# A hybrid attention and mixture-of-experts block: the attention's order of work, its score buffers and the form of eight output products

## The reference, cut to what matters

```
h    = rmsnorm(x) @ w_in                     # split: 4 x 512 columns for the recurrence, 3 x 512 for the attention
o_a  = head_rmsnorm(hgrn2(...)) * silu(hg)   # gated linear recurrence, 4 heads of 128
o_b  = head_rmsnorm(dilated_attention(...))  # 8 heads of 64, causal, softmax over masked scores
x    = x + concat(o_a, o_b) @ w_out          # w_out: 1024 x 1024
h2   = rmsnorm(x)
x    = x + top-4-of-32 experts(h2)           # each expert: 1024 x 2048 up, clamped SwiGLU, 1024 x 1024 down
out  = rmsnorm(x)
```

## Time and profile before

| | |
|---|---|
| median of 3 runs | 1307.71 us |
| the profiled execution's own time | 1308.46 us |
| its span, first to last instruction | 1306.6 us |
| PE busy, share of the span | 96% |
| DVE, ACT, POOL busy | 41%, 18%, 10% |
| granted TensorE clock, mean | 0.988 of full |
| data read from memory | 441.46 MB |

### The profile page before, as it was taken

One profiled execution on the slowest core, in us unless ns is written; L12 is line 12 of the kernel. 1 busy time (PEld: TensorE's weight loads), 2 busy tenths in 40 slices (PEclk: granted clock), 3 DMA queues, 4 the chain that ended last, 5 costly groups with the idle time before them and its releaser, 6 DMA issues.

```text
span 1306.6 us, 33478 instructions
## 1 busy us (share of the span) xinstructions
PE 1248.9 (96%) x14751; PEld 726.3 (56%) x14752; DVE 538.1 (41%) x1045; ACT 238.5 (18%) x485; POOL 135.8 (10%) x144
## 2 busy tenths in 40 slices
PE   6999999999999999999999999999999999999994
PEld 5888876675357565555444455444445454545442
DVE  5767646566424524223242333333333333242424
ACT  6364424421011111010010100010000000010102
POOL 0000001100022221221010101001010101010002
PEclk9999999998999999999999999999999999999997
DMA  9523219027899999999999999999999999999993
GB/s 294 163 65 91 72 45 408 2 114 300 348 395 417 423 415 423 411 415 424 424 424 423 424 424 422 426 422 422 423 424 423 423 424 424 424 423 425 424 390 141
DMA packets 69402, 450.87 MB, mean 345 GB/s; under 512 B 6921, under 2 KB 36077, under 8 KB 44576
## 3 DMA queue, kind: packets, MB, share of 16 engines
q1 hardware_dynamic: 64832, 438.59, 81.5%
q0 software_dynamic: 4416, 10.02, 2.4%
HBM read 441.46 MB, written 9.31 MB: 345 GB/s over the span
## 4 chain that ended last, share of the span: by engine, by line
PE 62%; DMA 32%; DVE 2%; issue 1%; ACT 1%; SPq 0%; DVEq 0%
DMA w_raw_pair<-w_down 29%; PE psum L1945 24%; PE psum L1963 14%; PE psum L1698 8%; PE psum L1695 3%; DMA w_raw_pair<-w_up 3%; PE psum L1974 2%; PE psum L1784 2%; PE psum L1832 1%; PE psum L1808 1%; PE psum L1936 1%; PE psum L1771 1%; PE psum L1849 1%; DMA x_rows<-x 1%; PE psum L2018 1%
## 5 line engine op out<-in xcount | busy, mean ns | idle before, releaser
L1945 PE MATMUL psum<-w_raw_pair,x_slots_turned 128*32 128x512 f32 x4928 | 550.4, 593 | 1.0 <-DMA w_raw_pair<-w_up 0.8
L1945 PEld LDWEIGHTS psum<-w_raw_pair,x_slots_turned 128*32 128x32 f32 x4928 | 208.8, 110 | 280.4 <-issue 218.9
L1963 PE MATMUL psum<-w_raw_pair,a_slots 128*32 128x256 f32 x4992 | 288.3, 380 | 11.7 <-DMA w_raw_pair<-w_down 10.6
L1963 PEld LDWEIGHTS psum<-w_raw_pair,a_slots 128*32 128x32 f32 x4992 | 186.3, 110 | 103.5 <-DMA w_raw_pair<-w_down 15.3
L1522 DVE TENSOR_TENSOR x_rows<-x_rows,psum 128x1024 f32<-128x1024 f32 x106 | 124.6, 1218 | 269.5 <-PE psum L1974 269.5
L845 ACT ACTIVATE lin<-psum 128x768 f32<-128x768 f32 (+1 forms) x32 | 22.5, 704 | 579.3 <-PE psum L1945 579.3
L1491 DVE STREAM_TRANSPOSE a_slots<-glu 128x768 f32<-128x768 f32 (+1 forms) x31 | 26.3, 849 | 202.6 <-PE psum L1963 202.6
L1486 DVE STREAM_TRANSPOSE x_slots_turned<-gathered_quarters 128x256 f32<-128x256 f32 x74 | 43.2, 628 | 113.7 <-PE psum L1945 113.0
L640 POOL COPY gather_quarters<-row_quarters 128x2 int32 (+1 forms) x30 | 16.4, 547 | 691.6 <-DVE x_slots_turned L1486 659.4
L1974 PEld LDWEIGHTS psum<-y_part_group,token_sel 32*128 32x128 f32 x2016 | 63.5, 184 | 42.7 <-issue 42.7
L645 POOL DMA_INDIRECT gathered_quarters<-normed_rows,gather_quarters x74 | 75.0, 1014 | 39.2 <-POOL gather_quarters L640 25.8
(11 more groups left out here) (290 smaller groups left out, 1045.9 us busy)
## 6 DMA issues: line engine op xcount, KB each, us to landing
w_raw_pair<-w_up SPq DMA_DIRECT2D x128, 2048.0 KB, 37.7
w_raw_pair<-w_down SPq DMA_DIRECT2D x64, 2048.0 KB, 37.9
w_in_raw<-w_in SPq DMA_DIRECT2D x28, 512.0 KB, 3.7
w_buf<-w_out SPq DMA_DIRECT2D x4, 1024.0 KB, 8.5
expert_rows<-zero_rows SPq DMA_DIRECT2D x5, 512.0 KB, 6.9
x_rows<-x SPq DMA_DIRECT2D x4, 512.0 KB, 5.2
x_rows<-x SPq DMA_DIRECT2D x1, 2048.0 KB, 17.4
normed_rows<-h_rows SPq DMA_DIRECT2D x4, 512.0 KB, 2.6
```

The source lines that it names most:

```text
L1945: ins = pe.matmul(U[quarter(j), g, :], slots, up_columns(w, j), start=False, stop=(c == UPC - 1))
L1963: ins = pe.matmul(banks[quarter(j), g, :], slots[:, g, 2 * c + h, :], raw[q.slot(m)][:, at_w:at_w + 256], start=False, stop=(c == DNC - 1 ...
```

## The change

1. **Early scores.** The scores of heads 0 and 1 (eight products) are made between `project("av", 0)` and `project("av", 1)`. Their masked maxima come on DVE right behind head 3's state scan; their exponentials on ACT behind the copies of `av` 0 and `av` 1.
2. **Three score buffers** in place of two. The scores of a pair are made in two parts (`scored_in`): tiles 0 and 1 in the turn before, tiles 2 and 3 in the turn of the even head. The statistics `mx`, `nmx`, `den`, `rden` have four places in place of two.
3. **Probabilities turned one head ahead.** In turn h, PE transposes head h+1 before it multiplies head h. ACT copies these in turn h and makes the exponentials of head h+2.
4. **Shares in three products.** ACT rounds the gate rows (`GH`, four copies) and `w_hgrn` (`WGH`, four of 128x1024) to fp32r, POOL makes both rests (`GLo`, `WOL[:, 0]`), and each share is twelve fp32r matmuls. Order: the even shares, then the odd ones; six in turns 2 to 7, one before `oT`, one behind it (`BEHIND_OT`), which the output products of the attention then follow.
5. **DVE waits for `x_again`** ahead of the loop over heads, not before share 0's add.
6. **Loads.** `WGH`, `GH` and the third score buffer lie where the weight pairs 1 and 2 of the ring go. SP issues pair 0 as before; the pairs 1 and 2 (`load_pair(FIRST, 2, ...)`, `load_pair(FIRST, 4, ...)`) wait for the share behind `oT`, and stand in SP's order ahead of the load of `G2`.

The core of the diff:

```diff
+            if g == "av":
+                jobs += [("qk", a, i) for i in range(TT) for a in (0, 1)]
...
+        def scored_in(h):
+            pair, tiles = ((h + 2) // 2, (2, 3)) if h % 2 == 0 else ((h + 3) // 2, (0, 1))
+            return ((2 * pair, 2 * pair + 1), tiles) if pair < AH // 2 else ((), ())
...
+        share_order = [n for half in range(2) for n in range(half, 2 * TT, 2)]
+        SHARES = dict(zip(range(2, AH), share_order))
+        BEFORE_OT, BEHIND_OT = share_order[AH - 2:]
+        W_HGRN_AFTER, W_OUT_AFTER = (0, 0, 1, 2), (3, 4, 5, 6)
+        jobs += pair_scores(-1) + [("pt", 0, c) for c in range(3)]
         for h in range(AH):
             if h in SHARES:
                 jobs += [("xa", SHARES[h])]
+            jobs += pair_scores(h)
+            if h + 1 < AH:
+                jobs += [("pt", h + 1, c) for c in range(3)]
             jobs += [("pv", h)]
+        jobs += [("xa", BEFORE_OT)] + [("oT", j) for j in range(4)] + [("xa", BEHIND_OT)]
...
 SP:
-            for n in range(0, 6, 2):
-                load_pair(FIRST, n, n, 0)
+            load_pair(FIRST, 0, 0, 0)
+            full(sp, "xa", BEHIND_OT)
+            load_pair(FIRST, 2, 2, 0)
+            load_pair(FIRST, 4, 4, 0)
             sp.wait_ge(S("attn_read"), AH)
             full(sp, "oT", 3)
             sp.dma_start(G2[:, :], norm2_g.to_broadcast([P, D])).then_inc(S("g2_in"), 16)
...
 ACT, in the recurrence's last head and behind it:
+                if h == HH - 1:
+                    exps(0)
                 projected(h, 1)
+                if h == HH - 1:
+                    exps(1)
...
+            probs_turned(0)
+            for h in range(HH):
+                freed(act, "gT", h)
+                act.activation(GH[:, h, :], G[:, h, :], ACT.Copy).then_inc(S("g_high"), 1)
+            for h in range(AH):
+                if h + 1 < AH:
+                    probs_turned(h + 1)
+                if h + 2 < AH:
+                    exps(h + 2)
+                    # then one rounding of w_hgrn (two in turn 0) or w_out
...
 DVE:
+            masked_max(2, (0, 1))
+            probs_turned(0)
+            masked_max(3, (0, 1))
+            dve.wait_ge(S("x_again"), 16)
+            for h in range(AH):
+                heads, tiles = scored_in(h)
+                if h in SHARES:
+                    add_share("xa", SHARES[h])
+                if heads:
+                    masked_max(heads[0], tiles)
+                if h + 1 < AH:
+                    probs_turned(h + 1)
+                if heads:
+                    masked_max(heads[1], tiles)
...
 PE, hgrn_share:
-                for k in range(HH):
-                    ins = pe.matmul(o, G[:, k, i * P:(i + 1) * P], Wb[:, 0, n % 2, k, :], start=(k == 0), stop=(k == HH - 1))
+                pe.wait_ge(S("g_low"), HH)
+                pe.wait_ge(S("w_hgrn_low"), 2 * half + 2)
+                for first, rows, w_rows in ((True, GH, WGH[:, half, :, :]), (False, GH, WOL[:, 0, half, :, :]),
+                                            (False, GLo, WGH[:, half, :, :])):
+                    for k in range(HH):
+                        ins = pe.matmul(o, rows[:, k, i * P:(i + 1) * P], w_rows[:, k, :], start=(first and k == 0), ...)
...
 PE, the loop:
+            scores(*scored_in(-1))
+            probs_turned(0)
+            for h in range(AH):
+                if h in SHARES:
+                    hgrn_share(SHARES[h])
+                scores(*scored_in(h))
+                if h + 1 < AH:
+                    probs_turned(h + 1)
+                # then pv of head h
```

More of the change, by code:

```diff
@@ L792, in end_rows, with exps @@
                                ).then_inc(free_sem("kdT", h), 1)
+            def exps(h):
+                for i in range(TT):
+                    act.wait_ge(S("neg_max"), max_number(h, i))
+                    s, n = E[h % 3][:, EOFF[i]:EOFF[i] + P * (i + 1)], TT * (h % 4) + i
+                    act.activation(s, s, ACT.Exp, bias=nmx[:, n:n + 1], scale=DH ** -0.5, accum_out=den[:, n:n + 1]
+                                   ).then_inc(S("probs"), 1)
             for h in range(HH):
@@ L805, in _, with probs_turned @@
                 projected(h, 3)
[L806 to L814, removed]
+            def probs_turned(h):
+                for c in (0, 2):
                     full(act, "pt", h, c)
@@ L1107, in scaled, with masked_max @@
                     dve.tensor_tensor(buf[:, b, :], buf[:, b, :], by[:, h, :], ALU.mult).then_inc(S("qk_scaled"), 1)
+            def masked_max(h, tiles):
+                for i in tiles:
+                    full(dve, "qk", h, i)
+                    n = TT * (h % 4) + i
+                    if h >= 3:
+                        full(dve, "pt", h - 3, 2)
+                    dve.tensor_tensor_reduce(E[h % 3][:, EOFF[i]:EOFF[i] + P * (i + 1)], bank("qk", h, i)[:, 0:P * (i + 1)],
+                                             cst("pairs")[:, (TT - 1 - i) * P:], 1.0, -3e38, ALU.add, ALU.max,
+                                             mx[:, n:n + 1]).then_inc(free_sem("qk", h, i), 1)
+                    freed(dve, "qk", h, i)
+                    dve.tensor_scalar(nmx[:, n:n + 1], mx[:, n:n + 1], -DH ** -0.5, None, ALU.mult
+                                      ).then_inc(S("neg_max"), 1)
             dve.wait_ge(S("c_rest"), 16)
@@ L1153, in _ @@
                     w_low(18 + 4 * h)
+                else:
+                    masked_max(0, range(TT))
+                    masked_max(1, range(TT))
                 dve.wait_ge(S("o_sq"), h + 1)
@@ L1170, in _ @@
                 dve.tensor_tensor(G[:, h, :], bank("gT", h), G[:, h, :], ALU.mult).then_inc(free_sem("gT", h), 1)
[L1172 to L1184, removed]
             def add_share(*name):
@@ L1231, in _ @@
             head_norm(range(AH - 2, AH))
[L1232 to L1233 removed]
+            add_share("xa", BEFORE_OT)
             for j in range(4):
@@ L1704, in _, with scores @@
                     project(g, j)
+            def scores(heads, tiles):
+                for i in tiles:
+                    for g in heads:
+                        r = slice(DH * (g % 2), DH * (g % 2) + DH)
+                        pe.matmul(begin("qk", g, i)[:, 0:(i + 1) * P], AQ[r, g // 2, i * P:(i + 1) * P],
+                                  AK[r, g // 2, 0:(i + 1) * P], start=True, stop=True).then_inc(full_sem("qk", g, i), 1)
             def hgrn_inputs(h):
@@ L1734, in hgrn_inputs @@
                     project(BETWEEN[h], 0)
+                    for j in range(4):
+                        freed(pe, "aq", j)
+                        freed(pe, "ak", j)
+                    scores((0, 1), range(TT))
                 project(BETWEEN[h], 1)
```

106 lines of the change are left out of this document (47 added, 59 removed).

## The result

The changed kernel takes **1322.97 us** (median of 4 runs, 1321.81 to 1324.42), the kernel before 1306.7 in the same comparison (4 runs, 1304.42 to 1308.83): a ratio of 1.0126, interval 1.0109 to 1.0142, so 1.3% slower. Forecast were 1318.2 and a range of 1308 to 1324. The profiled execution took 1323.15 (span 1321.3, mean granted clock 0.981, before 0.988).

A forecast was written before the change was run, and what follows sets the result against it. The prediction took the moment PE starts the experts as the bound: with the waits for x and G2 it comes 10.5 us later, 1308.46 + 10.5 = 1319.0, less 0.75 gives 1318.2 us; range 1308 to 1324, own mechanism 1314 to 1322.

The forecast's parts named there:

- What bounds it: Expert stage: DMA stream runs at its rate once PE starts the experts, so the time moves one for one with that start.
- The wait for x: Ahead of DVE's loop over heads: x lands at 212.65 us behind w_out's loads, PE idles 12 us, share 0 starts at 222.1.
- The loop: Share 0 to the last head's values on PE: 38.96 us against 54.7, 14.4 per pair against 17.7, DVE and ACT fitting under PE.
- The low clock: PE's restart after the pause for x, before share 0: half clock costs 1.7 us, charged once, ends 0 and 3.4.
- The end of the attention: Last values (261.06) to output products (270.6): 5.0 + 1.75 + 2.73 us, making the output products 1.6 us later.
- G2: Load behind two weight pairs, before DVE's first output-product add: lands 13.7 us after issue, at 284.4; row mean 286.8, +10.5.
- The sum: Whole kernel: experts start 10.5 us later, 1308.46 + 10.5 = 1319.0, less 0.75 gives 1318.2 us.
- The first: Rival at G2's load: not held up by the pairs, lands by 275.9, only +1.6 is left, 1309.3 us; chance 0.13.
- the second: Rival at x's load: lands near 200, POOL's second rest (208.9) limits; 1296.1 us with G2 early, 1305.0 late; chance 0.11.
- The third: Rival: both waits and more, G2 at its upper end (+5) or half-clock restarts (+1.8 and more), 1323 to 1326 us; chance 0.12.

The follow-up runs named there:

- e1: The changed kernel with DVE's wait for x_again moved from ahead of the loop to just before the first share is added: 1309.88 us, 1.0018 of before.
- f4: The kernel before with DVE waiting for x_again ahead of its loop over heads: 1325.38 us, 1.0144 of before.
- f2: The changed kernel with the load of x issued ahead of w_out's four loads, DVE's wait kept ahead of the loop: 1312.56 us, 1.0041 of before.
- f1: The changed kernel with 64 extra matmuls, read by nobody, behind head 0's values to fill PE's pause: 1321.11 us, 1.0107 of before.
- e2: The changed kernel with G2's load issued ahead of the last share's wait and of weight pairs 1 and 2: 1314.0 us, 1.0047 of before.
- f6: The kernel before with weight pairs 1 and 2 issued behind oT 3 and ahead of G2: 1317.48 us, 1.0079 of before.
- e3: The changed kernel with x_again waited for at the first share and G2 loaded ahead of the pairs (e1 and e2 together): 1301.73 us, 0.9948 of before.
- e4: The changed kernel with 54 extra matmuls, read by nobody, behind head 0's values to fill PE's pause: 1323.93 us, 1.0118 of before.

## Why the prediction was right, and what it mis-sized

The time, 1322.97, lies in the range of 1308 to 1324, but 1.0 us above the 1314 to 1322 that the prediction gave to its own mechanism and 4.8 above its sum. Both waits are shown; the step that was mis-sized is the low clock, below.

**What bounds it.** Right. The experts' start moves the end one for one: from there to the span's end it is 987.0 to 988.5 us in all thirteen kernels, whose starts lie between 305.56 and 334.58.

**The wait for x.** Right in place, cause and size. Foretold were w_out's loads at 192.95, x at 212.65, PE idle for 12 us; the profile has 193.68, 213.33 and 12.3. e1 takes this wait away and gets 13.1 us back; f4 puts it into the kernel before and pays 17.7. f2 keeps the wait, lets x land early and gets 10.4.

**The loop.** Right that the three-product order is cheaper per pair and that DVE and ACT fit under PE: no PE wait is left in it from 228 us to the end of the last values. From share 0 to there the sum gave 38.96 us; it took 42.5 (224.80 to 267.3). Of the 3.5 more, 2.4 are share 0 at half clock (5.23 for 2.81), the rest the pieces, each a little longer than priced (turnings with scores behind them 1.24 for 1.10, a share 2.81 for 2.73). One figure beside the sum is off: 54.7 less 38.96 is 15.8 us, not "some 14"; nothing is worked out from it.

**The low clock: the term that was too small.** "I charge 1.7 once (ends 0 and 3.4)". It cost about 6 us, more than the upper end: 6.1 by the differences below, 6.5 by the pieces. The four pieces in the chain up to the end of share 0 took 13.8 us (2.07 + 2.32 + 4.16 + 5.23); at full clock they take about 7.3, an estimate from the same pieces later in this trace (1.24, 2.18, 2.81) and half of 2.07. The prediction had the pause, but let the clock come back as in the earlier trace rows, after one product of scores. So share 0 came at 224.80 for 222.1 (0.7 of it is x itself, 2.0 the clock, on top of the 1.7), and then ran at half clock, 2.4 more. f1, which keeps the clock, has share 0 at 221.42 in 2.96 us, as priced. The output products start at 276.8 for 270.6: 0.7 + 2.0 + 2.4 + 1.1 = 6.2. The reason given, "the new pause is longer", isn't the right one either: in f2 idle times of 0.84 and 1.78 us brought the same four pieces at the same length.

**The end of the attention.** Right: from the last values to the output products 9.5 us (267.3 to 276.8), as summed.

**G2.** Right. It lands 14.3 us after the output products' start (foretold 13.7 to 13.8), DVE's idle time before its first add is 13.4, and the row mean comes 2.1 us after the landing (2.4). By itself this is +0.3 us. e2 takes this away and gets 9.0 us; f6 alone costs 10.6. The Trainium skill, "DMA: Bandwidth & Descriptors", section "Queues, rings and completion order", has each DMA engine take the descriptors of one queue's ring in order; the runs agree: the same 0.5 MB took 4.2 us alone, 13.15 and 14.47 behind 4.2 MB.

**The sum.** The row mean is 16.9 us later than before (foretold 10.5; 6.2 of the difference from above), the experts 15.7: sixteen matmuls ahead of them took 3.22 us before, at a mean clock of 0.57, and 1.96 after, at 1.00, which gives 1.2 back. The experts' own stage is 1.0 us shorter, so the profiled execution is 14.7 us longer (foretold 10.5), the median 16.3. The last 1.6 lie between the medians and one execution of each; no step accounts for them.

**The rivals.** The first (G2 not held up) and the second (x lands early) are refuted by the landings. The third, "each restart at half clock on the path", is what was added to mine, and the time lies between my range and its 1323 to 1326. The second's limit, POOL at 208.9, is real all the same: e1 runs into it at 209.59. Its two times, 1305.0 without the wait for x and 1296.1 without both, were 4.9 and 5.6 us too low (e1 1309.88, e3 1301.73). They too left out the low clock, which took 3.2 us in e1 and 2.7 in e3; what the rest is was not separated.

## What to carry to other kernels

Before a wait moves up an in-order engine, ask what is queued behind it, and read when its transfer lands, not when it was asked for: a transfer that ended a 2 us idle time before is a 15 us wait when its consumer comes 10 us earlier and it lands 3 us later. A small load goes ahead of the big ones in its queue. An expensive step for cheaper products pays only where the preparation (here POOL's rests) has time: the same edit couldn't be told from nothing where its first product stood in turn 2, and was worth 4.6 us a turn later. After an idle time of PE, price what follows at half clock as well as at full, even behind 2 us.

## What the runs showed of the hardware

- **The clock did not come back with the work.** PE's pause ended at 213.98; from 216.24 it worked without a gap of note, in scores, turnings and products of 64 columns, and the granted clock stayed at 0.50 up to some 229.9, 5 us into the first share. In f4 it is 0.50 for 212 to 220 with PE busy throughout. Why it stays low so long wasn't separated; f1 shows only that it can be held.
- **A gap of 2 us can be enough.** The clock fell to 0.50 during or behind idle times of PE of 0.84 and 1.78 us (f2), 1.70 (e4), 2.25 (e3) and 2.26 (e1). But it doesn't always: ahead of the turning of the rows PE is idle for 2.11 us in the changed kernel, e1, e3 and f1 alike, and the clock fell behind it in e1 and f1 only, each with one trace. What decides wasn't separated.
- **Landing time goes by what is queued ahead.** 2 MB: 8.3 us first (f2), 17.3 behind 4.2 MB. 0.5 MB: 3.7 (e2) and 4.2 with nothing ahead, 13.2 to 14.5 behind 4.2 MB. Worked out from these, it is some 2 to 2.5 us more per MB ahead.
